# Four SBUF buffers of a 256-token fp32 network start at other offsets within 128 bytes

## The chip, the cores and the metric

The kernel runs on one core of a Trainium2 chip. The metric is the device time of one execution in microseconds (us), and lower is better. Before the change it is 2893.67 us, the median of three runs (2886.39 to 2897.18).

## What is computed

The reference sends one activation of 256 tokens by 1024 features through seven residual layers of three families: two blocks with native-sparse and sliding-window attention, one block with a hybrid of block attention and an mLSTM, and four blocks with stick-breaking attention, a short convolution and gated linear attention. Around each mixer stand normalisations and feed-forward networks, and these hold most of the work:

```python
def swiglu(x, w_gu, w_down):                       # six times, hidden width 2816
    g, u = jnp.split(x @ w_gu, 2, axis=-1)
    return (jax.nn.silu(g) * u) @ w_down
def squared_relu_mlp(xn, w_up, w_down):            # four times, hidden width 4096
    return jnp.square(jax.nn.relu(xn @ w_up)) @ w_down
def stick_breaking_mixer(xn, w_qkv, w_o):          # a mixer: product in, heads, product out
    qkv = (xn @ w_qkv).reshape(b, s, 3, SB_HEADS, SB_HEAD_DIM)
    ...
    return o @ w_o
```

All of it is fp32, 500 MB of weights are read once, and every large product is wanted at more precision than one pass of the matrix unit in its reduced fp32 format (`F32R`) gives.

## The kernel before

**Split products.** Each operand of a large product is split into a high part rounded to `F32R` and a low part, the remainder. A product is then three matmuls: high by high, high by low, low by high. ScalarE makes the high parts (`split_hi`, line 329), VectorE the low parts (`split_lo`, line 336).

**Feed-forward stages.** A stage runs over units of weights: a 1 MB unit of the input weights (`ring_in`, split into `in_hi` and `in_lo`, two buffers each) and a 0.5 or 1 MB unit of the output weights (`ring_down`, split into `down_hi` and `down_lo`). In the input product the weights are the stationary operand (128 by 128, loaded by an LDWEIGHTS ahead of each matmul) and the normalised, transposed activation `feat` is the moving operand. For the gated networks this is L1099, L1100 and L1101, each with 256 moving columns, 48 matmuls a unit; for the squared-relu ones it is L1097 (512 columns: `feat` high and low together) and L1098 (256 columns), 32 a unit. In the output product the hidden activation (`hid_hi`, `hid_lo`) is stationary and `down_hi` or `down_lo` moves past it with 512 columns: L1169, L1170 and L1171, 12 a unit in the gated networks and 24 in the others. The loop runs 22 units in a gated stage (11 turns of two) and 16 in a squared-relu stage.

**Which activation buffer.** A `Feed` that follows a `Linear` writes its activation to a second place, `feat2_hi` and `feat2_lo`, at the end of the arena; so two of the six gated stages (the second feed-forward of each of the first two blocks) read `feat2` and the other four read `feat`. The profile calls the second place `feat_hi` and `feat_lo`.

**Linear stages.** In `Linear` (L1455 to L1457) the activation is stationary and the weights `in_hi` and `in_lo` move, 512 columns. In some input products of the mixers (L1985 to L1987 are the largest such group) the roles are as in the gated networks, with 256 columns. The output product of the hybrid mixer, L3816 to L3818, is a `Linear` whose activation lies half in `feat`, half in `hyb_hi` and `hyb_lo`.

**Order of the work.** Each engine runs its own program, stage after stage, and semaphores tie them; nothing reorders it. The weights come by SP's DMA queue. In three of the gated stages (the first feed-forward of both first blocks, and the second of the second block) GpSimd also computes a part of a modulation vector for a later block (`ModPart`).

**Where the buffers lie.** All are allocated in `Core.__init__`, one behind the other, each start rounded up to 32 bytes. Every slice that a large matmul reads starts a multiple of 512 bytes from the start of its buffer, so the start decides its place within 128 bytes.

| buffer | operand | start in a partition, before | within 128 B, before | within 128 B, after |
|---|---|---|---|---|
| `feat` | moving, or stationary in Linear | 47,968 | 96 | 32 |
| `in_hi`, `in_lo` | stationary, or moving in Linear | 64,352 and 80,736 | 96 | 0 |
| `ring_in`, `act`, `row` | split sources, not read by the products | 97,120 and on | 96 | 0 |
| `hid_hi`, `hid_lo` | stationary | 139,424 and 143,520 | 32 | 64 |
| `ring_down`, `proj` | source of the split; attention | 123,040 | 32 | 64 |
| `down_hi`, `down_lo` | moving | 147,744 and 164,128 | 32 | 96 |
| `feat2_hi`, `feat2_lo` | moving | 205,088 and 213,280 | 32 | 96 |
| `hyb_hi`, `hyb_lo` | stationary | 214,304 and 199,296 | 32 and 0 | 96 and 64 |

Of the kernel before, what the change touches and what calls it, by code (L numbers as in the profile page):

```python
# [116 lines left out]
    return slice(n * BLK, (n + 1) * BLK)  # L117


class Signal:  # L120


# [15 lines left out]
class Core:  # L138


    def __init__(self, nc, ctx, dram):
        self.nc, self.dram = nc, dram

        def sb(name, *shape):
            return ctx.enter_context(nc.sbuf_tensor(name, [P, *shape], F32))
# [4 lines left out]
        def split(name, *shape):  # L150
            return ctx.enter_context(nc.sbuf_tensor(name, [P, *shape], F32R))

        self.sb, self.sig = sb, sig
        self.const = sb("const", CONST_N)
        self.cols = sb("cols", COL_N)
        self.x = sb("x", TT, D)
        self.y = sb("y", TT, D)

        self.feat = split("feat", 2, KC, TOKENS)
        self.feat_hi, self.feat_lo = self.feat[:, 0], self.feat[:, 1]  # L160
        self.in_hi = split("in_hi", RING, UNIT)
        self.in_lo = split("in_lo", RING, UNIT)
        self.ring_in = sb("ring_in", RING, UNIT)
# [3 lines left out]
        self.fold = sb("fold", TT, P)  # L167
        self.minus_half = sb("minus_half", 8)
        self.eps = sb("eps", 8)
        at = nc.sbuf_base  # L170
        self.proj = sb("proj", TT, PROJ_COLS)


        def placed(name, offset, dtype, *shape):
            return nc.alloc_sbuf_tensor_at(name, [P, *shape], dtype, offset=offset)
# [3 lines left out]
        self.hid_hi = placed("hid_hi", at, F32R, RING, 2 * TOKENS)  # L179
        at += 4 * RING * 2 * TOKENS  # L180
        self.hid_lo = placed("hid_lo", at, F32R, RING, 2 * TOKENS)
        at = nc.sbuf_base
        self.arena = sb("arena", ARENA)
        self.down_hi = placed("down_hi", at, F32R, RING, UNIT)
# [6 lines left out]
        at = nc.sbuf_base - 4 * 2 * KC * TOKENS  # L191
# [4332 lines left out]
```

## Time and profile before

| | |
|---|---|
| median of the three runs | 2893.67 us |
| the profiled execution, by its span | 2889.2 us |
| TensorE (PE) busy | 2775.3 us, 96% |
| weight loads (PEld) busy | 2446.4 us, 85% |
| VectorE (DVE) busy | 1903.6 us, 66% |
| ScalarE (ACT) busy | 1201.3 us, 42% |
| GpSimd (POOL) busy | 609.9 us, 21% |
| mean DMA rate | 173 GB/s |

The profile gives no time for its execution besides the span, which lies between the lowest and the median run. A matmul's record overlaps the next one's, so its duration is not what it costs: the cost is the distance from its start to the start of the next.

### The profile page before, as it was taken

The numbers are of one execution on the slowest core, as the hardware profiler recorded it, in microseconds if no ns is written. First come the engines' busy times: TensorE is split into PE (matmuls) and PEld (weight loads), VectorE is DVE, ScalarE is ACT, GpSimd is POOL, SyncE is SP. The second block draws the span as 40 slices with busy tenths as digits, with TensorE's granted clock in tenths as the row PEclk, the third lists the DMA queues.
The fourth block names the chain that finished last, engine by engine and source line by source line (L and its number), as shares of the span: only waits on it lengthen the run. The fifth ranks groups of instructions, "written<-read, shape, count | busy, mean of one in ns | idle before, by whom it ended". The sixth has DMA issues, their size and how long they took to land.

```text
span 2889.2 us, 43862 instructions
## 1 busy us (share of the span) xinstructions
PE 2775.3 (96%) x17408; PEld 2446.4 (85%) x17408; DVE 1903.6 (66%) x2046; ACT 1201.3 (42%) x1478; POOL 609.9 (21%) x510
## 2 busy tenths in 40 slices
PE   8999999999989999999899999999899989999998
PEld 7997789999878988988699897888788878888887
DVE  6985656688867885555655556666666657655665
ACT  4343443343444334334444345334433444435433
POOL 6953300068434861000100000000000320000000
PEclk9999999999999999999999999999999999999999
DMA  7745134557526664443355434544554345533542
GB/s 278 265 183 163 45 145 189 186 215 275 184 73 225 254 241 175 180 147 103 110 184 186 146 132 178 196 157 160 194 195 163 118 145 197 197 126 116 211 187 103
DMA packets 126466, 500.31 MB, mean 173 GB/s; under 512 B 11025, under 2 KB 12337, under 8 KB 92961
## 3 DMA queue, kind: packets, MB, share of 16 engines
q1 hardware_dynamic: 112768, 450.39, 42.8%
q0 software_dynamic: 13600, 48.60, 4.9%
q8 instruction: 65, 1.06, 0.2%
q14 instruction: 33, 0.26, 0.0%
HBM read 497.90 MB, written 1.05 MB: 173 GB/s over the span
## 4 chain that ended last, share of the span: by engine, by line
PE 74%; DVE 13%; issue 6%; ACT 3%; POOL 2%; DMA 1%; DVEq 0%; SPq 0%; ACTq 0%; POOLq 0%
PE duo L1097 7%; PE duo L1169 7%; PE duo L1170 7%; PE duo L1171 7%; PE duo L1099 6%; PE duo L1100 6%; PE duo L1101 6%; PE duo L1098 4%; DVE down_lo L336 3%; PE duo L1455 3%; PE duo L1457 3%; PE duo L1456 3%; DVE in_lo L336 3%; ACT in_hi L329 2%; DVE hid_hi L1279 1%
## 5 line engine op out<-in xcount | busy, mean ns | idle before, releaser
L336 DVE TENSOR_TENSOR in_lo<-ring_in,in_hi 128x2048 fp32r<-128x2048 f32 x296 | 706.5, 2387 | 306.1 <-ACT in_hi L329 305.9
L329 ACT CAST in_hi<-ring_in 128x2048 fp32r<-128x2048 f32 (+1 forms) x293 | 554.5, 1893 | 276.8 <-PE duo L1457 152.3
L1169 PE MATMUL duo<-down_hi,hid_hi 128*128 128x512 f32 x1040 | 412.4, 397 | 10.9 <-DVE hid_lo L1281 7.5
L1170 PE MATMUL duo<-down_lo,hid_hi 128*128 128x512 f32 x1040 | 409.7, 394 | 0.0
L1171 PE MATMUL duo<-down_hi,hid_lo 128*128 128x512 f32 x1040 | 409.5, 394 | 0.0
L1099 PE MATMUL duo<-feat,in_hi 128*128 128x256 f32 x1408 | 400.1, 284 | 6.5 <-DVE in_lo L336 6.1
L1100 PE MATMUL duo<-feat,in_hi 128*128 128x256 f32 x1408 | 399.3, 284 | 0.0
L1101 PE MATMUL duo<-feat,in_lo 128*128 128x256 f32 x1408 | 399.1, 283 | 0.0
L336 DVE TENSOR_TENSOR down_lo<-ring_down,down_hi 128x1024 fp32r<-128x1024 f32 (+1 forms) x196 | 373.1, 1904 | 34.4 <-ACT down_hi L329 34.4
L1097 PE MATMUL duo<-feat,in_hi 128*128 128x512 f32 x1024 | 360.4, 395 | 0.0
L329 ACT CAST down_hi<-ring_down 128x1024 fp32r<-128x1024 f32 (+1 forms) x196 | 260.2, 1328 | 73.3 <-PE duo L1171 72.1
L1098 PE MATMUL duo<-feat,in_lo 128*128 128x256 f32 x1024 | 284.3, 278 | 0.0
L1099 PEld LDWEIGHTS duo<-feat,in_hi 128*128 128x128 f32 x1408 | 270.5, 192 | 11.2 <-DVE in_lo L336 6.1
L1100 PEld LDWEIGHTS duo<-feat,in_hi 128*128 128x128 f32 x1408 | 270.9, 192 | 3.2
L1101 PEld LDWEIGHTS duo<-feat,in_lo 128*128 128x128 f32 x1408 | 270.8, 192 | 0.0
L1169 PEld LDWEIGHTS duo<-down_hi,hid_hi 128*128 128x128 f32 x1040 | 196.0, 188 | 55.8 <-issue 16.0
L1171 PEld LDWEIGHTS duo<-down_hi,hid_lo 128*128 128x128 f32 x1040 | 195.7, 188 | 45.8
L1097 PEld LDWEIGHTS duo<-feat,in_hi 128*128 128x128 f32 x1024 | 192.0, 188 | 45.6 <-DVE in_lo L336 0.5
L1170 PEld LDWEIGHTS duo<-down_lo,hid_hi 128*128 128x128 f32 x1040 | 196.1, 189 | 37.2
L908 POOL TENSOR_TENSOR small<-small,minus_half 128x1 f32<-128x1 f32 x16 | 8.9, 554 | 1024.6 <-DVE small L941 1024.3
L3122 POOL TENSOR_TENSOR mod_sum<-mod_sum,mod_w 128x1024 f32<-128x1024 f32 x63 | 210.1, 3335 | 5.3
L1219 ACT ACTIVATE act<-act 128x256 f32<-128x256 f32 x88 | 36.8, 418 | 416.9 <-DVE act L1269 416.9
(487 smaller groups left out, 5286.0 us busy)
## 6 DMA issues: line engine op xcount, KB each, us to landing
ring_in<-in_ffn_in SPq DMA_DIRECT2D x196, 1024.0 KB, 6.4
ring_down<-in_ffn_down SPq DMA_DIRECT2D x132, 512.0 KB, 3.5
ring_down<-in_ffn_down SPq DMA_DIRECT2D x64, 1024.0 KB, 4.8
mod_w<-in_w_ada POOLq DMA_DIRECT2D x72, 512.0 KB, 5.2
ring_in<-in_sb_w_qkv SPq DMA_DIRECT2D x24, 1024.0 KB, 5.1
ring_in<-in_conv_w_in SPq DMA_DIRECT2D x12, 1024.0 KB, 5.2
ring_in<-in_gla_w_in SPq DMA_DIRECT2D x12, 1024.0 KB, 5.1
ring_in<-in_nsa_w_in SPq DMA_DIRECT2D x10, 1024.0 KB, 5.3
```

What stands on the lines that cost most here:

```text
L329: act.copy(hi[:, s, 0:n], raw[:, s, 0:n]).then_inc(hi_ready.sem, 1)
L336: dve.tensor_tensor(lo[:, s, 0:n], raw[:, s, 0:n], hi[:, s, 0:n].bitcast(F32), ALU.subtract).then_inc(lo_ready.sem, 1)
L1097: pe.matmul(out.rearrange("p (s n) -> p s n", s=2), hi, k.feat[:, :, c, :], start=c == 0, stop=False, skip_group_check=True)
L1098: return pe.matmul(out[:, 0:TOKENS], lo, k.feat_hi[:, c, :], start=False, stop=(c == KC - 1), skip_group_check=True)
L1099: pe.matmul(out, hi, self.feat_hi[:, c, :], start=opens, stop=False, skip_group_check=True)
L1100: pe.matmul(out, hi, self.feat_lo[:, c, :], start=False, stop=False, skip_group_check=True)
L1101: return pe.matmul(out, lo, self.feat_hi[:, c, :], start=False, stop=(c == KC - 1), skip_group_check=True)
L1169: pe.matmul(out, k.hid_hi[:, j, rows], k.down_hi[:, s, cols], start=opens, stop=False)
L1170: pe.matmul(out, k.hid_hi[:, j, rows], k.down_lo[:, s, cols], start=False, stop=False)
L1171: return pe.matmul(out, k.hid_lo[:, j, rows], k.down_hi[:, s, cols], start=False, stop=closes)
L1455: pe.matmul(out, f_hi, w_hi[:, c, :], start=(h == 0 and c == 0), stop=False)
L3122: pool.tensor_tensor(total, total, mod.w[:, s, :], ALU.add).then_inc(mod.used.sem, 1)
```

## The change

A helper `phase(name, at)` allocates a gap so that the next buffer starts at a chosen offset within 128 bytes. It is called four times: ahead of `feat` (offset 32), `in_hi` (0), `proj` with the hidden buffers behind it (64), and the arena with the output weights and `feat2` in it (96). The gaps take 192 bytes of each partition in all. Every engine's list of instructions is the same before and after, in the same order; only the addresses in them differ.

```diff
+LINE = 128
+FEATURE_PHASE, WEIGHT_PHASE, HIDDEN_PHASE, ARENA_PHASE = 32, 0, 64, 96
 ...
+        def phase(name, at):
+            gap = (at - nc.sbuf_base) % LINE
+            if gap:
+                sb(name, gap // 4)
 ...
+        phase("feature_gap", FEATURE_PHASE)
         self.feat = split("feat", 2, KC, TOKENS)
         self.feat_hi, self.feat_lo = self.feat[:, 0], self.feat[:, 1]
+        phase("weight_gap", WEIGHT_PHASE)
         self.in_hi = split("in_hi", RING, UNIT)
         self.in_lo = split("in_lo", RING, UNIT)
         self.ring_in = sb("ring_in", RING, UNIT)
 ...
+        phase("hidden_gap", HIDDEN_PHASE)
         at = nc.sbuf_base
         self.proj = sb("proj", TT, PROJ_COLS)
 ...
+        phase("arena_gap", ARENA_PHASE)
         at = nc.sbuf_base
         self.arena = sb("arena", ARENA)
         self.down_hi = placed("down_hi", at, F32R, RING, UNIT)
```

## Rows read from the trace of the kernel before

**Rows 1.** The page: busy time, share of the span and instructions.
```profile
PE 2775.3 (96%) x17408; PEld 2446.4 (85%) x17408; DVE 1903.6 (66%) x2046; ACT 1201.3 (42%) x1478; POOL 609.9 (21%) x510
```

**Rows 2.** Table by stage of three gated stages: columns in the header row.
```profile
core 0: us, PE busy (x) PEld busy (x) DVE busy (x) ACT busy (x) POOL busy (x), PEclk, DMA share, GB/s
16.35:208.70 192.35, 191.81 (x1331) 179.72 (x1332) 162.56 (x139) 72.34 (x71) 145.66 (x80) 1.00 0.67 249
...
884.22:1078.80 194.58, 187.17 (x1332) 173.18 (x1331) 167.96 (x144) 76.55 (x75) 140.28 (x80) 1.00 0.69 251
1094.80:1284.40 189.60, 189.60 (x1327) 176.77 (x1326) 102.91 (x120) 74.75 (x73) 0.00 (x0) 1.00 0.49 178
```

**Rows 3.** Groups of PE instructions: line, names, shapes, count, busy us, mean ns, idle.
```profile
L1169 PE MATMUL duo<-down_hi,hid_hi 128*128 128x512 f32 x1040 | 412.4, 397 | 10.9 <-DVE hid_lo L1281 7.5 <-DVE hid_lo L1296 3.1
...
L1099 PE MATMUL duo<-feat,in_hi 128*128 128x256 f32 x1408 | 400.1, 284 | 6.5 <-DVE in_lo L336 6.1 <-DVE feat L615 0.5
...
L1097 PE MATMUL duo<-feat,in_hi 128*128 128x512 f32 x1024 | 360.4, 395 | 0.0
...
L1099 PE MATMUL duo<-feat_hi,in_hi 128*128 128x256 f32 x704 | 196.2, 279 | 0.1
...
L1455 PE MATMUL duo<-in_hi,feat 128*128 128x512 f32 x432 | 172.5, 399 | 3.7 <-DVE in_lo L336 3.6
...
L1985 PE MATMUL duo<-feat,in_hi 128*128 128x256 f32 x256 | 72.6, 284 | 0.0
```

**Rows 4.** PE in order of time, gated units on `feat`: start us, us, instruction.
```profile
119.25 0.28 PE L1099 MATMUL duo<-feat,in_hi 128*128 128x256 f32 x1
...
121.03 0.28 PE L1099 MATMUL duo<-feat,in_hi 128*128 128x256 f32 x1
...
124.15 0.28 PE L1101 MATMUL duo<-feat,in_lo 128*128 128x256 f32 x1
...
127.77 0.28 PE L1099 MATMUL duo<-feat,in_hi 128*128 128x256 f32 x1
```

**Rows 5.** The same, gated units on `feat2`, without and with GpSimd's work.
```profile
448.62 0.28 PE L1099 MATMUL duo<-feat_hi,in_hi 128*128 128x256 f32 x1
...
451.01 0.28 PE L1099 MATMUL duo<-feat_hi,in_hi 128*128 128x256 f32 x1
...
453.96 0.28 PE L1101 MATMUL duo<-feat_hi,in_lo 128*128 128x256 f32 x1
...
456.87 0.28 PE L1099 MATMUL duo<-feat_hi,in_hi 128*128 128x256 f32 x1
...
937.89 0.28 PE L1099 MATMUL duo<-feat_hi,in_hi 128*128 128x256 f32 x1
...
946.34 0.28 PE L1099 MATMUL duo<-feat_hi,in_hi 128*128 128x256 f32 x1
```

**Rows 6.** The same, a squared-relu unit: its two halves and the next.
```profile
1846.76 0.39 PE L1097 MATMUL duo<-feat,in_hi 128*128 128x512 f32 x1
...
1852.31 0.39 PE L1169 MATMUL duo<-down_hi,hid_hi 128*128 128x512 f32 x1
...
1857.88 0.39 PE L1097 MATMUL duo<-feat,in_hi 128*128 128x512 f32 x1
```

**Rows 7.** The same, a Linear stage on `feat`, and the hybrid's on `hyb`.
```profile
1752.08 0.39 PE L1455 MATMUL duo<-in_hi,feat 128*128 128x512 f32 x1
...
1753.44 0.39 PE L1455 MATMUL duo<-in_hi,feat 128*128 128x512 f32 x1
...
1410.03 0.39 PE L3816 MATMUL duo<-in_hi,hyb_hi 128*128 128x512 f32 x1
...
1416.89 0.39 PE L3816 MATMUL duo<-in_hi,hyb_hi 128*128 128x512 f32 x1
```

**Rows 8.** Waits from 884 to 1079 us: who for whom, us, times, longest.
```profile
PE duo L1169 <- DVE hid_lo L1281: 5.9, 7, 1.7
```

## The prediction

> **What bounds the kernel.** I read the busy line first: PE is busy 96% of the span and its weight loads 85%, DVE 66% [rows 1]. The table by stage comes next. A gated stage without GpSimd's extra work has PE busy for all of its 189.60 us, at the full clock of 2.4 GHz (granted 1.00), with DVE busy 102.91 us and the DMA share at 0.49 [rows 2]. So it is bound by the rate at which matmuls start, and every nanosecond of start-to-start distance is a nanosecond of the span. The stages with GpSimd's work have DVE busy 162.56 of 192.35 us and 167.96 of 194.58 us [rows 2]: there DVE is a near second.
>
> Then the order in time, because the mean of a matmul record (284 ns) says nothing of its cost. From 121.03 to 124.15 us there are 26 distances: 3.12 us / 26 = 120.0 ns for a matmul of 256 columns on `feat` [rows 4]. The same instructions on `feat2` take, from 451.01 to 453.96 us, 2.95 / 26 = 113.5 ns [rows 5]. Nothing else differs there: same lines, shape, weights buffer and clock. What differs is where the moving operand lies. I call "distance" the moving start less the stationary start, modulo 128 bytes. `feat` and `in` both start at 96, distance 0; `feat2` starts at 32, distance 64. In whole units: 127.77 - 119.25 = 8.52 us at distance 0 [rows 4]; 456.87 - 448.62 = 8.25 us, and 946.34 - 937.89 = 8.45 us in the other stage, both at distance 64 [rows 5]. Distance 64 thus has two steady paces, and both beat distance 0. This is the whole basis for expecting anything from a change of addresses. One caution belongs to it: `feat2` is also 140 KB away from the weights where `feat` is 16 KB away, so the trace does not prove that the 128-byte place does it.
>
> **The change, part by part.** No instruction is added, removed or moved, no wait changes, and the operands keep their sizes. The only cost or gain is in the start-to-start distance of matmuls whose two operands now lie otherwise. After the change the distances are: `feat` over `in` 0 to 32; `feat2` over `in` 64 to 96; `down` over `hid` 0 to 32; weights over activation in Linear 0 to 96. No 256-column row of the trace stands at 32 or 96, so each term is bounded by the nearest rows.
>
> *Gated units on `feat`* (1408 matmuls of each of three lines [rows 3] at 16 per unit = 88 units, in four stages). Best case: the pace of the fast `feat2` unit, 8.25 us. Nearest two rows: 8.25 and 8.45 us; I take their middle, 8.35, since 32 lies between the 0 and the 64 that are measured. That is 0.17 us a unit. Two of the four stages have DVE at half load [rows 2]: 44 x 0.17 = 7.5 us. The other two carry GpSimd's work. The stage on `feat2` with that work shows what follows when the matmuls get faster there: it takes 194.58 us, more than the 192.35 us of the slower `feat` pace [rows 2], and PE waits seven times for DVE's hidden low part, 5.9 us [rows 8]. What is late next is DVE. I count half of the gain there: 3.7 us. Term: -11 us. Ends: -24 us (88 x 0.27), and on the bad side a loss as large as the gain that 64 shows, +24 us.
>
> *The same form in the mixers' input products* (L1985 to L1987, 3 x 256 [rows 3], and three smaller groups that I leave at nothing): 0.17 us / 48 = 3.5 ns each, 768 x 3.5 = 2.7 us. Term -3, ends -5 and +5.
>
> *Gated units on `feat2`* (704 / 16 = 44 units [rows 3]). They leave a distance that is known to be good. At 8.35 us, the stage now at 8.25 loses 22 x 0.10 = 2.2 us; the one now at 8.45 is held by DVE and gains nothing. Term +2. Ends: -2, and +8 if both fall to 8.52 (22 x 0.27 + 22 x 0.07).
>
> *Squared-relu input halves* (1024 / 16 = 64 units [rows 3]). From 1846.76 to 1852.31 us the 16 pairs take 5.55 us, 347 ns a pair [rows 6]. A pair of one 512- and one 256-column matmul at distance 0; if one of the two gets the 3.5 ns, 64 x 16 x 3.5 = 3.6 us. Term -4, ends -13 (12 ns a pair, twice the gain of 6.5) and +7.
>
> *Output products* (3 x 1040 [rows 3]). From 1852.31 to 1857.88 us, 24 matmuls in 5.57 us: 232.1 ns each [rows 6]. Linear's matmuls, of the same width, take (1753.44 - 1752.08) / 6 = 226.7 ns at the same distance 0 [rows 7], so 5 ns are there to be had, yet distance is not what separates those two rows. The hybrid's Linear on `hyb`, at distances 64 and 96, takes (1416.89 - 1410.03) / 30 = 228.7 ns [rows 7]. I take 1.5 ns: 3120 x 1.5 = 4.7 us, less what DVE hides. Term -4, ends -16 and +10.
>
> *Linear* (3 x 432 [rows 3] and smaller groups). It moves from distance 0 at 226.7 ns to 96, where the nearest row is the 228.7 ns of `hyb`: 1296 x 2.0 = +2.6 us. Term +2, ends 0 and +10. Here the trace argues against the change.
>
> DVE, ACT and the DMAs also see other addresses (the split of `down` reads and writes at different places where both were at 32), but they have slack in most stages; I cost this at nothing, and if DVE's splits grew by 1% it would show only in the three stages with GpSimd's work, as 1 to 2 us each.
>
> Sum: -11 - 3 + 2 - 4 - 4 + 2 = -18 us. Against the profile's span of 2889.2 us this is 2871; the median of the runs is 4.5 us above the span, so I forecast 2893.67 - 18 = 2876 us.
>
> The Trainium skill, page "SBUF — State Buffer", section "Who interferes with whom", says that TensorE has two independent read ports, one for the moving operand and one for the weight load, and that it never waits for anyone. By that rule the placement would change nothing at all. The trace disagrees in part: the 120.0 against 113.5 ns above are the same instructions at the same clock [rows 4, 5]. The page "TensorE: Matmul & The Clock Gate", section "Back-to-back issue gap", gives columns / 2.4 + 2.5 ns for an isolated matmul, 109 and 216 ns here; by this estimate every form of the kernel has 4 to 16 ns above its floor, and a placement that took all of it would bring more than I forecast.
>
> **The rivals.**
>
> *No effect.* The 6.5 ns between `feat` and `feat2` come from something else than the place within 128 bytes: the larger distance, or the higher address bits, which the change leaves nearly as they are (gaps of 32 to 96 bytes). For it: Linear at distance 0 (226.7 ns) is not slower than at 64 and 96 (228.7 ns) [rows 7], and distance 0 gives 232.1 ns in one place and 226.7 in another [rows 6, 7]. Against it: the 256-column form is steady at one pace over each unit, as a fixed relation of two streams would make it. Time: 2894.
>
> *32 apart is worse than 0 and 64.* If the two streams of reads meet in a pattern, a quarter of the period may be where each meeting costs most. The place is the 256-column input matmul and its weight load. The price: `feat` matmuls go from 120.0 to, say, 122 ns (the 2.0 ns that Linear loses away from 0), 4224 + 768 matmuls: +10 us; the `feat2` ones lose their advantage and go from 113.5 to 122, 2112 x 8.5 = 18 us, less the 5.9 us that DVE already takes: +12; Linear +3; output products +0 to +6. Together +28, so 2922. It decides from about 121 ns on: above it nothing of the list is left that gains. For it: `feat2` loses a place known to be good, and Linear's rows. Against it: both measured paces away from 0 in this form are faster.
>
> *The full gain.* All 256-column matmuls reach 113.5 ns, the relu pairs lose 12 ns, the output products come to Linear's 227 ns: -24 - 5 - 13 - 15, less some 10 us that DVE takes back: -47, so 2847. For it: all four relations leave 0 or keep away from it. Against it: no row shows output products below 228 on average.
>
> **How the numbers follow.** My forecast's case, a partial gain of 8 to 35 us: 0.47, with its own range 2859 to 2886. Full gain 0.11. No effect, or gains and losses that cancel: 0.22. Worse: 0.20. A measurement here can tell about 0.5%, 14.5 us, from no change. Of the forecast's case about 0.36 lies beyond that and 0.11 within. Faster: 0.36 + 0.11 = 0.47. Same: 0.11 + 0.22 = 0.33, less 0.02 that I give to small losses: 0.31. Slower: 0.20 + 0.02 = 0.22. The range reaches down to the full gain and up into the worse case: 2846 to 2912.
>
> **What would show it.** Start-to-start in a gated unit on `feat`: 113 to 118 ns if I am right, 120.0 again if the place does not matter, over 121 for the worse case. Unit length of the `feat2` stage near 450 us: 8.35, not 8.25. Waits for the hidden low part in the stages with GpSimd's work: longer than 5.9 us in sum. Output products at 230 to 231 ns and Linear at 228 to 229. DVE's and ACT's durations unchanged. I am wrong in the mechanism if the gain comes from the output products while the 256-column form stays at 120.0.

## The result, and the profile after

The change makes the kernel slower by 0.27%: 2901.03 us (median of nine runs, 2891.92 to 2907.47) against 2892.7 us for nine runs of the kernel before, a ratio of 1.0027 with the 95% interval 1.0017 to 1.0037. That is +8 us where -18 was forecast. It lies within the 0.5% that I called no change, but its sign is certain: the interval excludes 1.

The profiled execution of the changed kernel took 2891.92 us, the shortest of the nine; TensorE's granted clock averaged 0.990 in it, against 0.986 in the profile of before and 0.983 to 0.988 in the other eight. The traces have TensorE at the lower of its two clock levels for 60 us of it, against 80 us before. So the two spans, 2889.2 and 2890.1 us, differ by less than the medians, and the comparison is made by stages at full clock and by start-to-start distances.

The page's busy line, to be held against [rows 1], and its groups of TensorE instructions, against [rows 3] (lines moved down by 13):

```profile
PE 2776.7 (96%) x17408; PEld 2436.4 (84%) x17408; DVE 1905.5 (66%) x2046; ACT 1201.6 (42%) x1478; POOL 611.3 (21%) x510
...
L1182 PE MATMUL duo<-down_hi,hid_hi 128*128 128x512 f32 x1040 | 414.6, 399 | 11.2 <-DVE hid_lo L1294 7.8
...
L1112 PE MATMUL duo<-feat,in_hi 128*128 128x256 f32 x1408 | 395.9, 281 | 7.6 <-DVE in_lo L349 7.2
L1110 PE MATMUL duo<-feat,in_hi 128*128 128x512 f32 x1024 | 360.3, 394 | 0.0
```

The counts are the same, DVE, ACT and POOL are busy as long as before within 0.3%. Nothing but TensorE changed, and even there the busy sum hides it: the gated line lost 4 us of record time and the output line gained 2.

The table by stage, columns as in [rows 2]: first stage, second and third feed-forward together, the feed-forward on `feat2` with GpSimd's work, the one on `feat` without it, a `Linear`, a squared-relu stage.

```profile
16.13:209.38 193.25, 190.11 (x1332) 176.78 (x1332) 165.59 (x139) 72.20 (x71) 145.34 (x80) 1.00 0.66 248
397.24:783.53 386.29, 379.78 (x2681) 352.84 (x2679) 287.19 (x296) 154.30 (x155) 143.38 (x82) 1.00 0.58 209
886.82:1080.50 193.68, 189.56 (x1332) 176.01 (x1331) 167.00 (x144) 76.42 (x75) 143.06 (x80) 1.00 0.69 252
1096.13:1283.77 187.64, 187.64 (x1326) 174.26 (x1325) 103.19 (x121) 75.11 (x74) 0.21 (x1) 1.00 0.50 181
1740.05:1762.32 22.27, 22.27 (x98) 17.94 (x96) 8.70 (x9) 7.84 (x10) 0.00 (x0) 1.00 0.51 185
1766.56:1948.41 181.85, 180.30 (x905) 151.17 (x904) 122.53 (x99) 73.50 (x62) 3.77 (x5) 1.00 0.47 178
```

Of before, [rows 2] has the first, third and fourth; the other three are these, and a fourth, an input product of a stick-breaking mixer, that experiment 16 needs:

```profile
397.90:779.43 381.53, 376.54 (x2681) 350.86 (x2679) 286.91 (x296) 154.22 (x155) 143.90 (x82) 1.00 0.58 212
1745.15:1766.81 21.66, 21.66 (x97) 17.94 (x96) 8.54 (x9) 7.85 (x10) 0.00 (x0) 1.00 0.52 185
1771.21:1952.14 180.93, 179.48 (x905) 150.71 (x904) 122.53 (x99) 73.41 (x62) 3.77 (x5) 1.00 0.47 180
...
2569.18:2644.04 74.86, 73.79 (x526) 68.86 (x524) 43.01 (x39) 32.70 (x31) 1.44 (x3) 1.00 0.53 174
```

The second and third feed-forward of that stretch by themselves, first the one on `feat2` before and after, then the one on `feat` with GpSimd's work after:

```profile
397.90:585.03 187.13, 185.24 (x1342) 172.56 (x1340) 117.39 (x147) 79.48 (x79) 2.03 (x3) 1.00 0.51 191
397.24:588.75 191.51, 189.71 (x1341) 176.63 (x1340) 117.41 (x147) 79.61 (x79) 2.03 (x3) 1.00 0.50 186
588.75:783.53 194.78, 190.08 (x1341) 176.21 (x1340) 169.77 (x150) 74.69 (x78) 141.36 (x79) 1.00 0.65 232
```

The two stages on `feat` without GpSimd's work gained: 2.0 us in the one shown (189.60 to 187.64), 0.6 us in the other (193.64 to 193.03, with 2.6 us of it at half clock after). The two on `feat` with that work did not: 192.35 to 193.25 and 194.40 to 194.78 us. A 0.9 us there is no more than the spread of this stage: with every matmul pace as before it took 192.08 us in experiment 2 and 193.51 in experiment 16. The stage on `feat2` without GpSimd's work lost 4.4 us, each of the four squared-relu stages 0.9, the `Linear` shown 0.6.

In order of time on TensorE, columns as in [rows 4]: a gated unit on `feat` and its output product, the same on `feat2`, a squared-relu unit, a `Linear`, and the hybrid's.

```profile
118.78 0.28 PE L1112 MATMUL duo<-feat,in_hi 128*128 128x256 f32 x1
...
124.41 0.39 PE L1182 MATMUL duo<-down_hi,hid_hi 128*128 128x512 f32 x1
...
127.22 0.28 PE L1112 MATMUL duo<-feat,in_hi 128*128 128x256 f32 x1
...
448.53 0.28 PE L1112 MATMUL duo<-feat_hi,in_hi 128*128 128x256 f32 x1
...
454.20 0.40 PE L1182 MATMUL duo<-down_hi,hid_hi 128*128 128x512 f32 x1
...
457.01 0.28 PE L1112 MATMUL duo<-feat_hi,in_hi 128*128 128x256 f32 x1
...
1405.78 0.39 PE L3831 MATMUL duo<-in_hi,hyb_lo 128*128 128x512 f32 x1
...
1415.03 1.17 PE L3854 MATMUL duo<-const,arena 128*128 128x1 f32 x10
...
1747.16 0.39 PE L1468 MATMUL duo<-in_hi,feat 128*128 128x512 f32 x1
...
1750.66 0.39 PE L1468 MATMUL duo<-in_hi,feat 128*128 128x512 f32 x1
...
1842.46 0.40 PE L1110 MATMUL duo<-feat,in_hi 128*128 128x512 f32 x1
...
1848.02 0.40 PE L1182 MATMUL duo<-down_hi,hid_hi 128*128 128x512 f32 x1
...
1853.64 0.39 PE L1110 MATMUL duo<-feat,in_hi 128*128 128x512 f32 x1
```

On `feat`, 48 matmuls take 5.63 us, 117.3 ns each (120.0 in [rows 4]); the whole unit 8.44 us (8.52). On `feat2`, 5.67 us, 118.1 ns (113.5 in [rows 5]), the unit 8.48 (8.25). Output products: (1853.64 - 1848.02) / 24 = 234.2 ns (232.1 in [rows 6]). The relu pairs: 5.56 us for 16, where [rows 6] has 5.55. `Linear`: 3.50 us / 15 = 233.3 ns (226.7 in [rows 7]); the hybrid's 9.25 / 40 = 231.2 (228.7 in [rows 7]).

PE's wait for the hidden low part in the stage of [rows 8], from 887 to 1081 us:

```profile
PE duo L1182 <- DVE hid_lo L1294: 2.9, 4, 1.1
```

It fell from 5.9 to 2.9 us: slower `feat2` matmuls meet DVE later, so that stage did not grow (194.58 in [rows 2], now 193.68). In the two stages on `feat` with GpSimd's work the same wait grew, from nothing to 2.2 us and from 1.7 to 2.7. In sum it stayed, 7.5 us in [rows 3] and 7.8 us in the line of L1182 above.

Over all matmuls of a form at full clock, leaving out those that waited, the mean start-to-start distances and what they are worth together:

| form | matmuls | before, ns | after, ns | us |
|---|---|---|---|---|
| gated on `feat` | 4224 | 119.8 | 117.5 | -9.7 |
| mixers, 256 columns | 1392 | 119.9 | 118.2 | -2.4 |
| gated on `feat2` | 2112 | 114.7 | 118.3 | +7.6 |
| relu pair | 1024 | 347.3 | 347.1 | -0.2 |
| output products | 3120 | 232.1 | 234.2 | +6.6 |
| Linear | 1632 | 227.4 | 233.4 | +9.8 |

The sum is +12, the measured difference +8; the rest is at least in part cover by waits, as in the stage above.

### The profile page after: what moved, and what is told of

It reads as the page before. It is cut to its first block, busy times and chain, and to the rows that moved or that the text cites. A ratio compares the mean times of both kernels' runs of the same rounds, so it can differ in the third digit from the quotient of the medians.

```text
span 2890.1 us, 43862 instructions
## 1 busy us (share of the span) xinstructions
PE 2776.7 (96%) x17408; PEld 2436.4 (84%) x17408; DVE 1905.5 (66%) x2046; ACT 1201.6 (42%) x1478; POOL 611.3 (21%) x510
## 4 chain that ended last, share of the span: by engine, by line
PE 71%; DVE 15%; issue 6%; ACT 4%; DMA 2%; POOL 2%; DVEq 0%; SPq 0%; ACTq 0%; POOLq 0%
PE duo L1110 7%; PE duo L1182 7%; PE duo L1184 7%; PE duo L1183 7%; PE duo L1112 5%; PE duo L1113 5%; PE duo L1114 5%; DVE down_lo L349 4%; PE duo L1111 4%; PE duo L1468 3%; PE duo L1470 3%; PE duo L1469 3%; DVE in_lo L349 3%; DVE hid_hi L1292 2%; ACT in_hi L342 2%
## 5 line engine op out<-in xcount | busy, mean ns | idle before, releaser
L1182 PE MATMUL duo<-down_hi,hid_hi 128*128 128x512 f32 x1040 | 414.6, 399 | 11.2 <-DVE hid_lo L1294 7.8
L1112 PE MATMUL duo<-feat,in_hi 128*128 128x256 f32 x1408 | 395.9, 281 | 7.6 <-DVE in_lo L349 7.2
L1113 PE MATMUL duo<-feat,in_hi 128*128 128x256 f32 x1408 | 394.7, 280 | 0.0
L1112 PEld LDWEIGHTS duo<-feat,in_hi 128*128 128x128 f32 x1408 | 265.7, 189 | 12.8 <-DVE in_lo L349 6.1
L1113 PEld LDWEIGHTS duo<-feat,in_hi 128*128 128x128 f32 x1408 | 265.5, 189 | 3.4
L1182 PEld LDWEIGHTS duo<-down_hi,hid_hi 128*128 128x128 f32 x1040 | 195.7, 188 | 57.5 <-issue 16.1
L1110 PEld LDWEIGHTS duo<-feat,in_hi 128*128 128x128 f32 x1024 | 192.2, 188 | 44.1 <-DVE in_lo L349 0.2
```

The source lines that it names most:

```text
L1110: pe.matmul(out.rearrange("p (s n) -> p s n", s=2), hi, k.feat[:, :, c, :], start=c == 0, stop=False, skip_group_check=True)
L1112: pe.matmul(out, hi, self.feat_hi[:, c, :], start=opens, stop=False, skip_group_check=True)
L1113: pe.matmul(out, hi, self.feat_lo[:, c, :], start=False, stop=False, skip_group_check=True)
L1182: pe.matmul(out, k.hid_hi[:, j, rows], k.down_hi[:, s, cols], start=opens, stop=False)
```

## The experiments

Theory A: a matmul's start-to-start distance depends on where its two operands start relative to each other, and the change moved four such relations, some to better and some to worse places. Rival B: it is not the relative place but the absolute address, the distance of the buffers, or the other engines. From here on "distance" is the moving start less the stationary start, in bytes, first modulo 128 as in the prediction; the runs then showed why that is not enough. A distance "modulo 256" is named as such. The kernels that run matmuls alone hold 0.5 in every operand (two of the expectations say zero). Their paces leave out the first matmuls of a block.

**1. sweep: the matmuls alone.** The network is replaced by blocks of the kernel's own forms on two regions, one distance after the other:

```diff
+            for p, ds in ((0, DISTANCES), (96, [0, 32, 64, 96])):
+                for rep in range(3):
+                    for d in ds:
+                        s, m = sta[:, p // 4:], mov[:, (p + d) // 4:]
+                        gated(pe, s, m)      # 48 of 256 columns
+                        linear(pe, s, m)     # 24 of 512, one PSUM bank for 12
+                        last = down(pe, s, m)  # 24 of 512, another bank every 3
```

> This kernel leaves the whole network out: it only runs the three forms of large matmul (48 gated ones of 256 columns, 24 of a Linear with 512 columns, 24 of an output product with 512 columns and another bank every 3) on one stationary and one moving region, at distances 0, 16, ... 112, 128 and 256 bytes, with all other engines idle; then at 0, 32, 64, 96 with both starts 96 bytes later. Theory A (two streams of reads of TensorE itself, moving operand and next weight load, meet in a pattern that depends on their distance modulo 128 bytes): the gated form shows 120.0 ns start to start at 0, 113.3 or 117.5 at 64, 117 to 119 at 32 and 96; Linear 227 at 0 and 232 to 235 at 96; 128 and 256 repeat 0; moving both by 96 changes nothing. Theory B (other engines' reads and writes cause it): with the other engines idle all distances show one pace, near 109 ns for 256 columns and 216 for 512. Theory C (the place counts modulo more than 128 bytes): 128 and 256 differ from 0.

Measured, ns from start to start, three repeats within 0.1:

| distance | 0 | 16 | 32 | 48 | 64 | 80 | 96 | 112 | 128 | 256 |
|---|---|---|---|---|---|---|---|---|---|---|
| 256 columns | 120.0 | 118.7 | 116.7 | 118.5 | 113.3 | 119.9 | 119.9 | 113.7 | 118.8 | 119.9 |
| 512 columns | 226.9 | 231.5 | 233.4 | 229.9 | 228.9 | 231.3 | 233.2 | 231.1 | 231.9 | 226.9 |

Both operands moved by 96 together: the same at 0, 32, 64 and 96 within 0.2 ns. With every other engine idle and both regions at fixed places, the distance alone moves the pace by up to 6.7 ns: A stands. The form that changes banks every three matmuls ran as `linear` at 0, 32, 64, 96 and 256 (226.7, 233.4, 228.9, 233.2, 226.7), so banks cost nothing. The table is jagged, and 128 is not 0: the period assumed in the prediction is wrong.

The trace shows more than the means. At 112 the first seven start-to-start distances of each block of 48 are 116 to 121 ns, and all later ones 113 or 114: a pace is entered after some matmuls and then kept. At 96 they run through a cycle of six, 119, 120, 117, 125, 116 and 123 ns, of which 120.0 is the mean. (The 113.7 of the table at 112 still has three of the first seven in it.)

**2. shift32: everything moved by 32 bytes, all distances kept.**

```diff
-FEATURE_PHASE, WEIGHT_PHASE, HIDDEN_PHASE, ARENA_PHASE = 32, 0, 64, 96
+FEATURE_PHASE, WEIGHT_PHASE, HIDDEN_PHASE, ARENA_PHASE = 0, 0, 64, 64
```

> All four groups of buffers start 32 bytes later within 128 than before (feat 0, in 0, hid and proj 64, arena 64), so that every distance between a moving and a stationary operand is as before. Theory A: paces as before, 120.0 and 227 and 232 ns, ratio 1.000 within 0.2%. Rival (the place of a buffer itself counts, or its place against the row constants and x, which don't move): paces as after the change, ratio about 1.003.

2893.7 us, ratio to before 1.001 [0.9999, 1.0021], every pace as before (within 0.3 ns). A shift of all buffers does not matter; B is out in the kernel too.

**3. feat64: `feat` over `in` alone changed; all else where it was before within 128 bytes, every other relation kept.**

```diff
+FEATURE_PHASE, WEIGHT_PHASE, HIDDEN_PHASE, ARENA_PHASE = 32, 96, 32, 32
```

> Only feat moves, to 32 within 128 bytes; all else keeps its place of before within 128 bytes, so feat over in stands at 64, Linear at 64, down over hid at 0 and feat2 at 64 as before. Theory A: 4224 + 1392 matmuls of 256 columns go from 119.8 to about 114.7 ns, -28 us, of which DVE takes some 5 back; Linear from 227.4 to about 229, +2: ratio to before 0.993. Rival (feat2 is fast because it lies far from the weights, not because of the distance modulo 128): 256 columns stay at 120.0 ns and the ratio is 1.000.

2885.11 us, 0.997 [0.9959, 0.998]: a gain, from the relation that `feat2` had, though not half of the 0.7% expected. Gated on `feat` 114.3 ns. In the table by stage, the gated stage without GpSimd's work and a squared-relu stage:

```profile
1098.03:1282.01 183.98, 183.98 (x1326) 171.01 (x1325) 103.51 (x121) 75.50 (x74) 0.71 (x2) 1.00 0.50 185
1758.74:1940.99 182.25, 180.78 (x906) 151.59 (x904) 122.56 (x99) 73.53 (x62) 3.77 (x5) 1.00 0.47 178
```

189.60 became 183.98; the first stage, with GpSimd's work and DVE as near second, stayed at 192.87 against 192.35. PE's wait for the hidden low part in it, of which the trace of before has none:

```profile
PE duo L1182 <- DVE hid_lo L1294: 4.7, 5, 1.7
```

That is the prediction's argument on DVE, and in this trace nothing of the gain is kept there. How much is kept in general one trace of each kernel does not settle: in all64, the next run, the stage took 190.59 us. The relu stage pays 1.3 us (pairs 352.3 ns).

**4. all64: every relation at 64 modulo 128.**

```diff
+FEATURE_PHASE, WEIGHT_PHASE, HIDDEN_PHASE, ARENA_PHASE = 64, 0, 0, 64
```

> The change's own helper with other offsets: feat 64, in 0, hid 0, arena 64, so that all four distances are 64: feat over in, feat2 over in, down over hid, and in over feat in Linear. Theory A: as the run with feat alone at 64 for all but the output products; those are the open term, 232 ns at distance 0 and 234 at 32: by Linear's rows at 64 (229) they would come to about 230, -6 us. Ratio 0.990 to 0.994. If distance 64 is worse than 0 for the output products as 32 is, 0.995 or more.

2893.58 us, 1.0006 [0.9994, 1.0018]: no change, where 0.990 to 0.994 was expected. Gated on `feat` 116.5 to 117.2 ns, on `feat2` 117.6, output products 233.2, Linear 229.2, and the relu pair 353. The same distance as in feat64 gave 116.8 instead of 114.3 ns; so one distance can have more than one pace.

**5. sweep2: a longer range.** As sweep, distances 0 to 512 in steps of 32, and the squared-relu pair as third form.

> Again only large matmuls on one stationary and one moving region with all other engines idle, the network left out: 48 gated (256 columns), 24 of a Linear (512), and 32 of the squared-relu form (512 columns in two pieces, then 256), at distances 0 to 480 in steps of 32, and 512. The first sweep gave other paces at 128 than at 0 and the same ones at 256. Theory A2 (the pattern repeats every 256 bytes, not every 128): 256 to 480 repeat 0 to 224, Linear is fast (226.9 ns) at 0, 256 and 512 alone and near 232 at 128. Rival (it repeats every 512 and 256 equals 0 by chance): some distance from 288 on differs from the one 256 below it. The squared-relu pair should show 347 ns at 0 and 352 at 64 or 192, as in the kernels.

The table repeats after 256 bytes: each value from 256 to 480 equals its partner from 0 to 224 within 0.1 ns. At 64 the 256-column form ran at 117.8 here and at 113.3 in sweep. There the block before stood at 48 in the first set and at 32, as here, in the second, with 113.3 in both; what differs is the form that ran before, the relu pair here and the bank-changing one there. In 512 columns only 0 is fast (226.9); the rest lie from 228.7 to 234.3. Relu, per matmul: 179.1 at 0, 175.4 at 32 and 160, 177.4 to 179.0 elsewhere.

Modulo 256 the kernel's relations read otherwise than the prediction had them:

| relation | before | after |
|---|---|---|
| `feat` over `in` | 0 | 160 |
| weights over activation in Linear | 0 | 96 |
| `down` over `hid` | 128 | 160 |
| `feat2` over `in` | 192 | 224 |

The four relations of all64 are, in the order of the table, 192, 64, 192 and 64: its 233.2 and 229.2 ns are what the two sweeps have at 192 and 64.

This also explains what [rows 6, 7] showed and I could not place: 232.1 and 226.7 ns "at the same distance 0" were 128 and 0.

**6. hid128: the hidden buffers alone moved by 128 bytes, `down` over `hid` from 128 to 0 modulo 256** (in the kernel before).

```diff
-        at += 4 * RING * UNIT
+        at += 4 * RING * UNIT + 128
```

> The kernel before with hid_hi and hid_lo alone moved on by 128 bytes: down over hid goes from 8320 to 8192 bytes, the same place within 128 bytes, another within 256 (128 to 0). Theory A2: 3120 output matmuls go from 232 to 226.7 ns, -16.5 us less what DVE takes back: ratio 0.994 to 0.996. Rival (128 bytes is the period, and output products are slower than Linear's for another reason, as their change of bank every 3 matmuls): 232 ns as before, ratio 1.000.

2889.42 us, 0.9986 [0.9977, 0.9996]. Output products 232.1 to 229.1 on average, 227 in the median; a unit's twelve:

```profile
125.27 0.40 PE L1169 MATMUL duo<-down_hi,hid_hi 128*128 128x512 f32 x1
...
128.02 0.28 PE L1099 MATMUL duo<-feat,in_hi 128*128 128x256 f32 x1
```

2.75 us / 12 = 229.2 ns. But the gated matmuls on `feat2`, whose two operands did not move, went from 114.7 to 117.3 ns: what runs before them chose their pace. That took back more than half: 3120 x 3.0 = 9 us won, 2112 x 2.6 = 5.5 us lost, and so 0.9986 where 0.994 to 0.996 was expected.

**7. feat64_hid128: both together.**

```diff
+FEATURE_PHASE, WEIGHT_PHASE, HIDDEN_PHASE, ARENA_PHASE = 32, 96, 32, 32
 ...
-        at += 4 * RING * UNIT
+        at += 4 * RING * UNIT + 128
```

> feat64 and hid128 together: feat over in at 64 within 128 (192 within 256), down over hid at 0 within 256. Theory A2: the gains add where PE sets the pace: 0.997 x 0.995 = 0.992, a little less where GpSimd's work holds DVE. If DVE already sets the pace of the gated stages, 0.995.

2887.93 us, 0.9975 [0.9965, 0.9985]: no better than feat64 alone. The gains did not add, as 0.992 had it. The output products kept theirs (229), the gated matmuls went to their second pace (117.5).

**8. feat32only and 9. arenaonly: the change in two halves.** The first changes the relation of `feat` to `in` only, the second only those of the output weights to the hidden buffers and of `feat2` to `in`; the buffers behind move along.

```diff
+FEATURE_PHASE, WEIGHT_PHASE, HIDDEN_PHASE, ARENA_PHASE = 32, 0, 64, 64   # feat32only
+FEATURE_PHASE, WEIGHT_PHASE, HIDDEN_PHASE, ARENA_PHASE = 0, 0, 64, 96    # arenaonly
```

> One part of the change alone: feat at 32 and in at 0 within 128 bytes as after it, but arena, hid and feat2 at their distances of before (down over hid 128 within 256, feat2 over in 192). By the paces measured in the two traces: 256-column matmuls on feat 119.8 to 117.5 ns (5616 x -2.2 = -12 us), Linear 227.4 to 233.4 (1632 x 6 = +10 us), output products and feat2 as before: -2 us, ratio 0.999 to 1.000. So the change's loss would come from its other half, the arena's place: +6.5 us for the output products and +7.6 us for feat2. Rival: the loss comes from Linear and is here in full, 1.003.

> The other part of the change alone: feat over in at distance 0 as before, hid and arena placed as after (down over hid 160 within 256, feat2 over in 224 within 256). From the paces of the two traces: output products 232 to 234.3 ns, 3120 x 2.2 = +7 us; feat2 114.7 to 118.3, 2112 x 3.6 = +7.6 us, of which a part is DVE's anyway; Linear on feat unchanged. Ratio 1.003 to 1.005: this half carries the loss. Rival (it was Linear on feat, +10 us): 1.000.

feat32only: 2893.37 us, 0.9994 [0.9985, 1.0003]. Gated on `feat` 118.0 ns, Linear 233.4: 5616 x 1.8 = 10 us won, 1632 x 6.0 = 10 us lost. arenaonly: 2908.05 us, 1.0056 [1.0043, 1.0069]. `feat2` 118.2 ns, output products 234.2, and the relu pair, whose operands it leaves at distance 0, 352.1 ns instead of 347.3. A squared-relu stage, 180.93 before:

```profile
1786.35:1969.33 182.98, 181.41 (x905) 151.22 (x904) 122.51 (x99) 73.43 (x62) 3.76 (x5) 1.00 0.47 177
```

So the loss comes with the second half and the gain of the first is eaten by Linear. The halves add up to +0.5%, the whole is +0.27%: the relu pair falls into a slower second pace in arenaonly and not in the changed kernel.

**10. columns: how wide is the stationary operand.** 128, 64 or 32 stationary columns at five distances.

```diff
+                    for cols in (128, 64, 32):
+                        wide(pe, s, m, cols)     # 24 of 512 moving columns
+                        last = narrow(pe, s, m, cols)  # 24 of 256
```

> Only matmuls, the network left out and other engines idle: 24 of 512 moving columns and 24 of 256, each with a stationary operand of 128, 64 or 32 columns, at distances 0, 32, 64, 128 and 192. Theory A2 says that what a matmul takes beyond its columns at 2.4 GHz is caused by the reads of the next weights, so it shrinks with the columns of the stationary operand: at 512 moving columns the 11 ns (distance 0) to 17 ns (128) above 216 become about half at 64 columns and a quarter at 32, and the differences between distances shrink with them. Rival (the cost hangs on the moving reads or the PSUM writes alone): the pace and its differences by distance are the same for 32 stationary columns as for 128.

| distance | 0 | 32 | 64 | 128 | 192 |
|---|---|---|---|---|---|
| 512 moving, 128 stationary | 228.3 | 233.3 | 228.7 | 232.7 | 233.5 |
| 512 moving, 32 stationary | 231.8 | 226.7 | 231.3 | 231.0 | 231.5 |
| 256 moving, 128 stationary | 120.0 | 116.6 | 117.8 | 118.6 | 117.8 |
| 256 moving, 32 stationary | 113.4 | 117.2 | 113.4 | 113.3 | 116.7 |

64 columns gave 228 to 233 and 113 to 119 ns. In the mean over the five distances 512 moving columns take 231.3, 230.2 and 230.5 ns with 128, 64 and 32 stationary ones, 256 take 118.1, 116.9 and 114.8. With 512 the cost does not shrink with the columns loaded; with 256 it shrinks, but what lies above the 109.2 ns of experiment 14 falls from 9 to 5.6 ns and not to a quarter. The idea that it goes in proportion to the bytes of the weight load falls; that they have a share in it at 256 columns does not.

**11. columns32 and 12. fixed32: does the distance or the program's place set it with 32 columns?** columns32 goes through eight distances; fixed32 stays twelve blocks long at 0, then 32, then 192.

```diff
+            for p, ds in ((0, list(range(0, 256, 32))), (96, [0, 32, 64, 128])):   # columns32, three times over
+            for p, ds in ((0, [0] * 12), (0, [32] * 12), (0, [192] * 12)):         # fixed32
+                        for cols in (32,):
```

> This kernel leaves the whole network out: it only runs blocks of TensorE matmuls on zero data, 24 of 512 moving columns and 24 of 256 at each distance (moving start less stationary start) from 0 to 224 bytes in steps of 32, with a stationary operand of 32 columns, and then with both starts moved by 96 bytes at distances 0, 32, 64 and 128. Theory 1, the two streams of reads meet by the distance between them alone: the second set repeats the first at each distance within 0.3 ns (512 columns: 231.8, 226.7, 231.3, 231.0 at 0, 32, 64, 128; 256 columns: 113.4, 117.2, 113.4, 113.3). Theory 2, the place of each operand by itself within 256 bytes sets the pace and a full stationary operand only hides that: the second set differs by 2 ns or more at one distance or more. Under both at least one of the eight distances gives 226.7 ns for 512 columns.

> This kernel leaves the whole network out: blocks of 24 matmuls of 512 and 24 of 256 columns, stationary operand of 32 columns, twelve blocks at distance 0, twelve at 32, twelve at 192. In the run with eight distances the paces of such blocks recurred every fourth block whatever the distance was (256 columns: 113.3, then 120.0 or 113.3, then 116.7 or 113.3, then 117.7). Theory A, the distance before decides: at a distance that stays there is one pace from the second block on. Theory B, with 32 stationary columns the place in the program or the time decides: the same sequence of four shows again at each of the three fixed distances.

columns32 does not decide between its theories, and 226.7 ns did not appear. Within it each distance of the first set has one pace in all three rounds, within 0.1 ns: from 0 to 224 the 256-column blocks take 113.3, 120.0, 116.7, 117.7, 113.3, 113.3, 113.3 and 117.8 ns, those of 512 columns 230.4 to 233.5 and, at 224, 239.3 ns, more than any distance gave with 128 stationary columns. The second set repeats 0, 32 and 64; at 128 it has 115.6 for 113.3 ns, but there the block before stood at 64 and not at 96. Against the run before, the same 32 columns at distance 32 take 120.0 and 233.5 ns instead of 117.2 and 226.7, with other blocks ahead of them. The pattern of every fourth block, from which the expectation of fixed32 starts, does not hold: 0 and 128, and 96 and 224, share a pace for 256 columns; 32 and 160, and 64 and 192, do not.

fixed32 rules out the place in the program: from its second block on each distance has one pace, 113.3 at 0, 120.0 at 32 and 113.3 at 192, and 231.7, 233.3, 231.1 for 512 columns, twelve times over within 0.1 ns. So the place in the program does not decide (theory A); that what ran before does is what is left, and the next run tests it with the kernel's own width.

**13. neighbours: the kernel's own 128 columns, every distance after every other.**

```diff
-DISTANCES = list(range(0, 512, 32)) + [512]
+DISTANCES = [32 * i for i in [0, 0, 1, 0, 2, 0, 3, 0, 4, ..., 7, 7, 0]]
```

> This kernel leaves the whole network out: it only runs blocks of TensorE matmuls on constant data (48 gated ones of 256 columns, then 24 of 512, stationary operand of 128 columns), 65 blocks whose distances are 0 to 224 bytes in steps of 32 in an order in which every distance follows every distance once, itself too. Theory 1, the distance sets the pace: each distance gives one pace in all of its blocks within 0.5 ns, those of the earlier sweep (256 columns: 120.0, 116.7, 117.8, 120.0, 120.0, 117.3, 113.3, 118.4; 512 columns: 226.8 at 0 and 228.8 to 234.3 elsewhere). Theory 2, a distance has a few steady paces and what ran before chooses: at least one distance takes two or more paces, 113.3 and 117.8 at 64 above all, and the choice goes by the distance before. Theory 3, the place in the program sets it: paces repeat by the block's number and not by its distance, and 0 is neither always 120.0 nor always 226.8.

| distance, modulo 256 | 0 | 32 | 64 | 96 | 128 | 160 | 192 | 224 |
|---|---|---|---|---|---|---|---|---|
| 256 columns, lowest | 119.8 | 116.7 | 113.3 | 119.7 | 118.6 | 117.3 | 113.3 | 118.3 |
| 256 columns, highest | 120.0 | 117.8 | 117.8 | 120.0 | 120.0 | 120.0 | 117.8 | 118.4 |
| 512 columns, lowest | 226.9 | 233.2 | 228.9 | 233.3 | 232.5 | 234.3 | 233.3 | 233.3 |
| 512 columns, highest | 226.9 | 233.4 | 228.9 | 233.3 | 233.3 | 234.4 | 233.3 | 233.3 |

Each cell is over eight predecessors. Theory 2 of that run holds for 256 columns: 0, 96 and 224 have one pace, the others two or more, and at 64 and 192 they are 4.5 ns apart: at 64 the fast one follows 32, 160 and 192, the slow one the other five. In order of time, a block at 64 that follows 32 (from 210.65) and one at 64 that follows 224 (from 333.97), 48 matmuls each; before them the 24 of 512 columns at distance 0 (from 36.54) and at 128 (from 115.16):

```profile
36.54 0.40 PE L42 MATMUL bank<-mov,sta 128*128 128x512 f32 x1
...
42.01 0.28 PE L32 MATMUL bank<-mov,sta 128*128 128x256 f32 x1
...
115.16 0.39 PE L42 MATMUL bank<-mov,sta 128*128 128x512 f32 x1
...
120.75 0.28 PE L32 MATMUL bank<-mov,sta 128*128 128x256 f32 x1
...
210.65 0.28 PE L32 MATMUL bank<-mov,sta 128*128 128x256 f32 x1
...
216.09 0.39 PE L42 MATMUL bank<-mov,sta 128*128 128x512 f32 x1
...
333.97 0.28 PE L32 MATMUL bank<-mov,sta 128*128 128x256 f32 x1
...
339.62 0.39 PE L42 MATMUL bank<-mov,sta 128*128 128x512 f32 x1
```

5.44 and 5.65 us for the same instructions at the same addresses: 113.3 and 117.7 ns. The 512-column blocks, 5.47 and 5.59 us.

This table gives the paces of the changed kernel without looking at it: `feat` at 160 117.3 or more (117.5 measured), `feat2` at 224 118.4 (118.3), output products at 160 234.3 (234.2), Linear at 96 233.3 (233.4). Only the relu pair's does not come out of the sweeps (twice 179.1 ns at 0 is 358, the kernel has 347).

**14. half_width: the same blocks with bfloat16 operands.**

```diff
-F32R = mybir.dt.float32r
+F32R = mybir.dt.bfloat16
```

> This kernel leaves the whole network out: the same blocks on zero data with bfloat16 operands of 2 bytes in place of the 4-byte reduced fp32, stationary operand of 128 columns, distances 0 to 224 bytes in steps of 32. Theory 1, the excess comes from the number of bytes that the two streams read (512 and 256 columns of 4 bytes against 128 of 4 bytes): with half the bytes the spread over the distances shrinks to half or less of what 4 bytes show, under 4 ns for 512 columns (where it was 7.6) and under 3.4 ns for 256 (where it was 6.8). Theory 2, the excess belongs to the order in which addresses are met, not to the bytes: the spread stays at 6 ns or more in both. Theory 3, it belongs to the 4-byte format alone: one pace at all distances, within 0.3 ns.

```profile
26.67 0.38 PE L31 MATMUL bank<-mov,sta 128*128 128x512 bf16 x1
...
31.85 0.27 PE L41 MATMUL bank<-mov,sta 128*128 128x256 bf16 x1
...
34.47 0.38 PE L31 MATMUL bank<-mov,sta 128*128 128x512 bf16 x1
```

5.18 us / 24 = 215.8 ns and 2.62 / 24 = 109.2 ns, at all eight distances within 0.1 ns, as theory 3 has it. With 2-byte operands the effect is gone; whether it belongs to the 4-byte format as such or to its number of bytes, this run does not separate. The Trainium skill, page "TensorE: Matmul & The Clock Gate", section "Back-to-back issue gap", gives columns / 2.4 + 2.5 ns for an isolated matmul: 215.8 and 109.2 ns. The bfloat16 trace agrees to the tenth of a nanosecond, though its matmuls stand in a stream with weight loads, for which that section has about 131 ns at 512 columns; no run here shows that. In the reduced fp32 format no run came below 226.7 and 113.3.

**15. views and 16. views2: each stage its own best place.** One buffer can't suit both roles: `feat` at 192 is good as moving operand (113.3 or 117.8) and bad as stationary one (`Linear` then stands at 64, 228.9). So the kernel before gets second names for the same memory, 192 bytes on for the stages behind `FeatTurn`, and 128 bytes on for the hidden buffers of the squared-relu stages; views2 adds the two stick-breaking input products.

```diff
+        sb("late_gap", 64)
+        self.late_feat = nc.alloc_sbuf_tensor_at("late_feat", [P, 2, KC, TOKENS], F32R, offset=feat_at + 192)
 ...
+        self.late_hid_hi = placed("late_hid_hi", at - 4 * RING * 2 * TOKENS + 128, F32R, RING, 2 * TOKENS)
+        self.late_hid_lo = placed("late_hid_lo", at + 128, F32R, RING, 2 * TOKENS)
 ...
+        self.hid_hi, self.hid_lo = (core.hid_hi, core.hid_lo) if silu else (core.late_hid_hi, core.late_hid_lo)
```

> The kernel before with a place per stage: a second view of feat 192 bytes on for the stages behind a FeatTurn (two gated stages without GpSimd's work, and the hybrid's input product), and a second view of hid 128 bytes on for the four squared-relu stages. All else as before. From the stage times of feat64 (-5.6, -3.5 and -2 us) and of hid128 (4 x -1.3): -16 us, ratio 0.9945. If the fast pace of the gated form is not entered (it has a second one near 117.5 ns at the same distance), -8 us, 0.997.

> views, with the second view of feat also for the two stick-breaking input products, whose 256-column matmuls outnumber their Linear ones: by feat64's stage times -4.4 and -1.2 us more, ratio 0.9925 to 0.994.

views: 2878.89 us, 0.9958 [0.9943, 0.9972], between the two values expected. views2: 2872.78 us, 0.9939 [0.9924, 0.9955], as expected, the fastest version and below both kernels. Its table by stage: a gated stage without GpSimd's work, a `Linear`, a squared-relu stage, the second stick-breaking input product.

```profile
1097.39:1280.94 183.55, 183.55 (x1327) 170.58 (x1326) 102.95 (x120) 74.78 (x73) 0.00 (x0) 1.00 0.50 184
1732.87:1754.54 21.67, 21.67 (x98) 17.94 (x96) 8.55 (x9) 7.84 (x10) 0.00 (x0) 1.00 0.52 184
1758.93:1938.59 179.66, 178.19 (x906) 150.55 (x904) 122.46 (x99) 73.47 (x62) 3.76 (x5) 1.00 0.48 181
2553.89:2626.62 72.73, 71.69 (x525) 66.60 (x524) 43.03 (x39) 32.75 (x31) 1.44 (x3) 1.00 0.55 178
```

Before they took 189.60, 21.66, 180.93 and 74.86 us. The gated stage has its 6 us, and Linear pays nothing for it.

## Why the prediction was wrong

The forecast was -18 us and +8 came. 2901 us lies inside the range of 2846 to 2912 all the same, but only because the range reached up into the worse case; no term of the forecast leads there, and that is luck.

The step that failed is the reading of a pace at a distance that no row had from the rows next to it, with the distance taken modulo 128. Step by step:

- *What bounds the kernel.* Right. The stages in which TensorE has no cover moved by their paces, and the time with them: the gated one shown by -1.96 us (1056 x -2.3 and 264 x +2.1 ns are -1.9), a `Linear` by 0.61 (96 x 6.0 ns is 0.6).
- *"The trace does not prove that the 128-byte place does it".* The place does it (sweep, shift32), but modulo 256. The rival of no effect falls.
- *Gated units on `feat`, "-11 us".* The sign of the pace was right, the size too large: 2.3 ns a matmul were won where 3.5 were counted, 9.7 us by pace. By time the four stages gained 1.3 us in sum, output products included: 2.0 and 0.6 us where DVE leaves room, nothing in the two with GpSimd's work. "I count half of the gain there" was too much in this trace and in that of feat64.
- *Gated units on `feat2`, "+2".* Mis-sized: +7.6 by pace. 8.35 us a unit was the mean of two measured units at one distance; the new distance has a pace of its own, 118.4 ns in the sweeps, and a unit of 8.48 us, above both. The stated end of +8 covers it.
- *Output products, "-4".* Wrong in sign: +6.6. Of all terms this one missed by most. The argument was that 232.1 and 226.7 ns stood at the same distance and 5 ns were to be had. They stood at 128 and 0 modulo 256, and 160 is the slowest place in the table. The buffers' starts in the table of the kernel before held this; I reduced them modulo 128 because the change does.
- *Linear, "+2".* Right in sign, a fifth of the size: +9.8. The 228.7 ns of `hyb` was one row with two operands at two distances (64 for two matmuls in three, 224 for the third, modulo 256). It mostly told of 64, where sweep has 228.9, and not of 96, where sweep has 233.2.
- *Squared-relu halves, "-4".* Nothing came (-0.2).
- *The waits for the hidden low part* were to grow beyond 5.9 us in sum. That number was of one stage; over the three it was 7.5 us and became 7.8. It grew on `feat`, where the matmuls got faster, and fell from 5.9 to 2.9 us on `feat2`, where they got slower.

One assumption lies under all of these: that between two measured distances the pace lies between the two measured paces. I wrote "since 32 lies between the 0 and the 64 that are measured". The sweep is jagged, 0 at 226.9 ns is a single good point between 233.3 on both sides, and interpolating it gave gains where there were losses. The rival "32 apart is worse than 0 and 64" was right in its sign, in `feat2` and in Linear, wrong that `feat` would lose; it decided from a `feat` pace of 121 ns on, while the loss came at 117.5. Of its +28 us the kernel lost 8.

The rule that I weighed in the prediction, two independent read ports and an engine that never waits for anyone (the Trainium skill, page "SBUF — State Buffer", section "Who interferes with whom"), would give 2894 us. The runs contradict it for this format: 113.3 to 120.0 and 226.7 to 234.4 ns by start offset and what ran before, with every other engine idle. For bfloat16 half_width agrees with it.

Why the pace depends on the distance in 4-byte operands stays open. The runs exclude the PSUM banks, the other engines, the absolute address, and a cost in proportion to the weights loaded. They leave a state of the two streams of reads that the distance allows and the preceding matmuls choose. The blocks of sweep that settle after seven matmuls fit it; no run shows the reads themselves.

## What to carry to other kernels

Where matmuls in the reduced fp32 format run back to back with 128 stationary columns, the start of the moving operand relative to the stationary one, modulo 256 bytes, is worth up to 6% of a 256-column matmul and 3% of a 512-column one. With 512 columns keep it at 0; with 256 columns 64 and 192 are best but can fall to 117.8 ns by what runs before, so measure in place. Take such a table by a sweep before choosing: no point of it follows from its neighbours, and one buffer in two roles may want two views.

## What the runs showed of the hardware that I had not expected

- The pace repeats with a period of 256 bytes (sweep2), and 128 differs from 0 by 5 to 7 ns in 512 columns.
- Two steady paces at one distance, 113.3 and 117.8 ns, kept over 48 matmuls and chosen by what ran before (neighbours, hid128).
- bfloat16 has neither: 109.2 and 215.8 ns everywhere (half_width), where the reduced fp32 format has 113.3 and 226.9 at its best. Its weight load record is 98 ns for 128 columns, against 190 ns in the reduced fp32 format (109 ns for 32 columns), yet with 32 columns more than one pace at one distance is still there (at 192, 116.7 ns in columns and 113.3 in columns32).
- A pace is not entered at once: in sweep, at 112, after seven matmuls.
